# Turning the expert inputs with 32x32 block transposes on VectorE in an MoE block

## The reference

```python
def clamped_swiglu_expert(xb, w_gu, b_gu, w_down, b_down):
    gu = xb @ w_gu + b_gu                      # (.., 1024) @ (1024, 2048)
    gate = jnp.minimum(gu[:, :D_FF], SWIGLU_LIMIT)
    up = jnp.clip(gu[:, D_FF:], -SWIGLU_LIMIT, SWIGLU_LIMIT)
    act = (up + 1.0) * (gate * jax.nn.sigmoid(gate * SWIGLU_ALPHA))
    return act @ w_down + b_down               # (.., 1024) @ (1024, 1024)
...
# top 4 of 32 experts for each token; the output is the gated sum over a token's 4 experts
```

## Time and profile before

| | |
|---|---|
| time of three runs, us | 1556.98, 1557.81, 1560.6 (median 1557.81) |
| span of the profiled execution, us | 1561.2 |
| TensorE busy in matmuls | 1331.3 us, 85% of the span |
| VectorE busy | 461.4 us, 30% |
| ScalarE busy | 237.5 us, 15% |
| GpSimd busy | 163.4 us, 10% |
| HBM read and written | 447.69 MB and 28.44 MB |

### The profile page before, as it was taken

One profiled execution on the slowest core, in us unless ns is written; L12 is line 12 of the kernel. 1 busy time (PEld: TensorE's weight loads), 2 busy tenths in 40 slices (PEclk: granted clock), 3 DMA queues, 4 the chain that ended last, 5 costly groups with the idle time before them and its releaser, 6 DMA issues.

```text
span 1561.2 us, 31310 instructions
## 1 busy us (share of the span) xinstructions
PE 1331.3 (85%) x12575; PEld 639.3 (41%) x12576; DVE 461.4 (30%) x1076; ACT 237.5 (15%) x514; POOL 163.4 (10%) x269
## 2 busy tenths in 40 slices
PE   7999969998689888878989999989889767998881
PEld 6754459955433333332333333323333222333330
DVE  1247695342322212222212222212222121221226
ACT  3145453421011000000000100000000000010000
POOL 3000040000410000000000100001000000100031
PEclk9999999999699999999999999999999988999985
DMA  8721002075699999999979899899979999969955
GB/s 304 232 73 61 21 35 55 2 297 225 260 353 379 403 376 418 400 388 370 393 316 391 335 368 355 338 404 416 389 315 413 417 416 398 399 279 402 402 216 201
DMA packets 117336, 476.85 MB, mean 305 GB/s; under 512 B 8388, under 2 KB 42228, under 8 KB 84532
## 3 DMA queue, kind: packets, MB, share of 16 engines
q1 hardware_dynamic: 99792, 444.50, 72.0%
q0 software_dynamic: 6816, 21.24, 3.7%
q10 hardware_dynamic: 10692, 10.62, 2.0%
HBM read 447.69 MB, written 28.44 MB: 305 GB/s over the span
## 4 chain that ended last, share of the span: by engine, by line
DMA 59%; PE 25%; DVE 6%; SPq 5%; issue 2%; another core or an unknown queue 1%; ACT 1%; ACTq 1%; DVEq 0%; POOLq 0%; POOL 0%
DMA y_scratch<-Y 55%; PE PS L749 14%; PE PS L1129 4%; PE PSC L749 3%; PE PS L1149 3%; DMA BDN<-in_expert_b_down 2%; DVE Y L1541 2%; SPq L297 2%; SPq L264 2%; DMA W<-in_w_in 1%; DVE W L1580 1%; SPq L279 1%; PE PS L979 1%; DMA XG<-hn_scratch,IDXC 1%
## 5 line engine op out<-in xcount | busy, mean ns | idle before, releaser
L1129 PE MATMUL PS<-W,XT 128*32 128x512 f32 x5184 | 602.4, 606 | 37.6 <-DVE GU L1521 30.5
L1149 PE MATMUL PS<-W,AT 128*32 128x256 f32 x5184 | 335.3, 411 | 112.0 <-ACT AT L710 106.6
L1129 PEld LDWEIGHTS PS<-W,XT 128*32 128x32 f32 x5184 | 160.9, 111 | 374.4 <-issue 364.1
L1149 PEld LDWEIGHTS PS<-W,AT 128*32 128x32 f32 x5184 | 176.0, 118 | 298.7 <-ACT AT L710 149.3
L749 PE MATMUL PS<-W 128*128 128x512 f32 (+6 forms) x1068 | 274.3, 415 | 9.9 <-DMA W<-in_w_in 4.0
L749 PEld LDWEIGHTS PS<-W 128*128 128x128 f32 (+1 forms) x1068 | 173.4, 196 | 90.9 <-issue 74.2
L1541 DVE TENSOR_TENSOR Y<-PS,BDN 128x256 f32<-128x256 f32 x81 | 34.4, 425 | 579.8 <-DMA y_scratch<-Y 552.2
L710 ACT ACTIVATE AT<-PS 128x256 f32<-128x256 f32 x81 | 31.1, 384 | 839.3 <-issue 597.4
L1521 DVE TENSOR_TENSOR GU<-PS,BGU 128x512 f32<-128x512 f32 x81 | 56.0, 692 | 195.5 <-PE PS L1129 180.2
L465 POOL COPY IDXC<-IDX 128x1 uint32 (+1 forms) x82 | 15.0, 183 | 929.1 <-PE PS L1110 923.4
L468 POOL DMA_INDIRECT XG<-hn_scratch,IDXC x82 | 80.1, 977 | 64.6 <-POOL IDXC L465 64.6
(11 more groups left out here) (238 smaller groups left out, 652.5 us busy)
## 6 DMA issues: line engine op xcount, KB each, us to landing
W<-in_expert_w_gate_up SPq DMA_DIRECT2D x128, 2048.0 KB, 13.5
W<-in_expert_w_down SPq DMA_DIRECT2D x64, 2048.0 KB
y_scratch<-Y ACTq DMA_DIRECT2D x79, 128.0 KB
W<-in_w_in SPq DMA_DIRECT2D x9, 1024.0 KB, 6.4
y_scratch<-AT SPq DMA_DIRECT2D x1, 8704.0 KB
W<-in_x SPq DMA_DIRECT2D x8, 512.0 KB, 4.9
y_last_scratch<-AT SPq DMA_DIRECT2D x1, 2560.0 KB, 39.2
W<-in_w_in SPq DMA_DIRECT2D x2, 1040.0 KB, 11.0
```

What stands on the lines that cost most here:

```text
L1129: last = pe.matmul(GPS[32 * j:32 * j + 32, :].rearrange("p (g n) -> p g n", g=2), XT[:, (k % 2) * P + (k // 2) * 32:(k % 2) * P + (k // 2) ...
L1149: last = pe.matmul(DPS[32 * j:32 * j + 32, :], AT[:, (k % 2) * P + (k // 2) * 32:(k % 2) * P + (k // 2) * 32 + 32], DNW[p][:, k, j * QW:(j ...
```

## The change

- XG is turned by one VectorE transpose of 32x32 blocks (x_turn) straight from SBUF to SBUF. It stands in activate(i), behind the clamp of the gate, and turns X of block i+1. The four TensorE transposes of a block and the two ScalarE copies are gone.
- The activations are turned in the same way at the end of activate(i), behind a wait until down(i-1) has ended, since AT is a single tile.
- The source is read with a stride of 8 elements, so that partition 32j + f of chunk c holds row 8(32j + f) + c. The weights therefore lie as (p k): partition p holds rows 8p to 8p + 7 of the matrix. What one copy puts in one partition (2 rows of 8 KB of gate-up, 4 rows of 4 KB of down) is now one run of 16 KB in HBM and in SBUF. The number of copies (6 for an expert) and their order and waits are as before.
- y_evac, y_store, the single tile Y and their waits are the same. The store is now not behind at_copy on ScalarE, and down(i) gets AT from VectorE.

```diff
+NC = QW // 32
...
-        GPS, DPS, XPS, ATPS, RPS = PS[0], PS[1][:, 0:QW], PS[2][:, 0:QW], PS[3][:, 0:QW], PS[6][:, 0:P]
+        GPS, DPS, RPS = PS[0], PS[1][:, 0:QW], PS[6][:, 0:P]
+        XGV = XG[:, :].rearrange("p (f c) -> p c f", c=NC)
+        XTV = XT[:, :].rearrange("p (c f) -> p c f", c=NC)
+        ACTV = GU[:, 0:QW].rearrange("p (f c) -> p c f", c=NC)
+        ATV = AT[:, :].rearrange("p (c f) -> p c f", c=NC)
...
-                                 w_gu[e].rearrange("(k p) n -> p k n", p=P)[:, 2 * q:2 * q + 2, :]).then_inc(S_(f"gu_in{p}{q}"), 16)
+                                 w_gu[e].rearrange("(p k) n -> p k n", p=P)[:, 2 * q:2 * q + 2, :]).then_inc(S_(f"gu_in{p}{q}"), 16)
...
-                                 w_dn[e].rearrange("(k p) n -> p k n", p=P)[:, 4 * q:4 * q + 4, :]).then_inc(S_(f"dn_in{p}{q}"), 16)
+                                 w_dn[e].rearrange("(p k) n -> p k n", p=P)[:, 4 * q:4 * q + 4, :]).then_inc(S_(f"dn_in{p}{q}"), 16)
...
             def next_gather(i):
-                g.wait_ge(S_("xt_ps"), i)
+                g.wait_ge(S_("xt_ready"), i)
...
             def block_step(i, dst, row):
-                at_copy(i - 1)
-                a.wait_ge(S_("xt_ps"), i + 2)
-                a.wait_ge(S_("gu_ps"), i + 1)
-                xt_copy(i + 1)
                 sigmoid(i)
                 y_store(i - 1, dst, row)
...
-                    if k == 5:
-                        pe.wait_ge(S_("gathered"), (i + 2) * 16)
-                        x_transposes(i + 1)
-                        if not first:
-                            pe.wait_ge(S_("act_ready"), i)
-                            act_transposes()
...
-                                         XT[:, (k % 2) * P + (k // 2) * 32:(k % 2) * P + (k // 2) * 32 + 32], rhs,
+                                         XT[:, 32 * k:32 * k + 32], rhs,
...
-                                         AT[:, (k % 2) * P + (k // 2) * 32:(k % 2) * P + (k // 2) * 32 + 32],
+                                         AT[:, 32 * k:32 * k + 32],
...
+            def x_turn(i):
+                v.wait_ge(S_("gathered"), (i + 1) * 16)
+                v.transpose(XTV, XGV).then_inc(S_("xt_ready"), 1)
             def activate(i, p, first):
                 v.wait_ge(S_("gu_ps"), i + 1)
                 if not first:
-                    v.wait_ge(S_("at_ps"), i)
+                    v.wait_ge(S_("at_ready"), i)
                 tt(GU[:, :], GPS, BGU[p][:, :], ALU.add).then_inc(S_("gu_evac"), 1)
                 v.wait_ge(S_("gu_evac"), i + 1)
                 ts(GU[:, 0:QW], GU[:, 0:QW], LIMIT, None, ALU.min).then_inc(S_("gate_ready"), 1)
+                x_turn(i + 1)
...
                 stt(out=GU[:, 0:QW], in0=GU[:, QW:2 * QW], scalar=1.0, in1=SIG[:, :], op0=ALU.add, op1=ALU.mult).then_inc(S_("act_ready"), 1)
+                v.wait_ge(S_("act_ready"), i + 1)
+                v.wait_ge(S_("d_ps"), i + 1)
+                v.transpose(ATV, ACTV).then_inc(S_("at_ready"), 1)
```

More of the change, by code:

```diff
@@ L339, in _ @@
                 sp.dma_start(GUW[0][:, 2 * q:2 * q + 2, :],
-                             w_gu[0].rearrange("(k p) n -> p k n", p=P)[:, 2 * q:2 * q + 2, :]).then_inc(S_(f"gu_in0{q}"), 16)
+                             w_gu[0].rearrange("(p k) n -> p k n", p=P)[:, 2 * q:2 * q + 2, :]).then_inc(S_(f"gu_in0{q}"), 16)
             for t in range(NT):
@@ L696, in _ @@
             nb = last + 1
-            def xt_copy(i):
-                a.activation(XT[:, :], XPS, ACT.Copy).then_inc(S_("xt_ready"), 1)
             def sigmoid(i):
@@ L705, in sigmoid @@
                 a.activation(SIG[:, :], GU[:, 0:QW], ACT.Sigmoid, scale=ALPHA).then_inc(S_("sig_ready"), 1)
[L707 to L710, removed]
             def y_store(i, dst, row):
@@ L718, in _ @@
             f = a.value_load(LASTB[0:1, NE - 2:NE - 1], min_val=NE - 2, max_val=MAXB - 1) + 1
[L719 to L723, removed]
             sigmoid(0)
@@ L741, in _ @@
                     block_step(f + 1 + j, yl_d, j * BT)
-            at_copy(last)
             y_store(last, yl_d, (last - f) * BT)
@@ L1104, in _ @@
                 last.then_inc(S_("list_ps"), 1)
[L1106 to L1111, removed]
             def gate_up(i, p, rnd, first_of_expert, first):
@@ L1133, in gate_up @@
                         last.then_inc(S_(f"gu_read{k // 2}" if k < KD - 1 else "gu_ps"), 1)
[L1135 to L1138, removed]
             def down(i, p, rnd):
@@ L1171, in _ @@
             pe.transpose(RPS, ident[:, :], ident[:, :]).then_inc(S_("d_ps"), 1)
-            x_transposes(0)
             gate_up(0, 0, 16, True, True)
@@ L1189, in _ @@
             last = expert(NE - 1, 1, last, NE * 8, NE * 8)
-            pe.wait_ge(S_("act_ready"), last + 1)
-            act_transposes()
             down(last, 1, NE * 8)
@@ L1543, in _ @@
             v.memset(IDXC[:, 1:2], 0).then_inc(S_("y_ready"), 1)
+            x_turn(0)
             spread_biases(0, 0, 32)
```

## The result

The changed kernel takes 1679.24 us (median; 1673.81 to 1683.27), the kernel before took 1557.5 us beside it. The ratio is 1.077, with a 95% interval of 1.074 to 1.081: 122 us slower. The profiled execution has a span of 1678.3 us, 117.1 us more than that of before.

A forecast was written before the change was run, and what follows sets the result against it. The prediction took waits for stores of Y as the bound, DMA engines second. Longer store waits added 212 us over 29 experts and VectorE transposes 5: span 1561.2 + 217 = 1778, median 1775 us, range 1600 to 1900.

The forecast's parts named there:

- Rival (a): Waits of store packets for weight pieces double in the expert stage: 1775 us, own range 1690 to 1890; chance 0.68.
- (b): Store packets wait longer, but weight loads fill the gaps: 1561 + 0 to 100, about 1620 us; chance 0.12.
- The ring and its price: y_evac, store, landing, next y_evac: each store packet waits for one weight piece, 0.65 us at 16 KB, store turn 26.3 us.
- Four engines with 33 packets: A store of Y, 132 packets, was read as four DMA engines with 33 packets each.
- The walk through an expert of two blocks: Step-by-step timing of stores against loads: 42 slow packets, 39.2 us for each expert; at best 33, at worst 42.4.
- Experts of three blocks: First store quick, the next two meet 26 and 14 weight pieces: 44.8 us for each of 13 experts.
- The start of the stage: The start of the expert stage, with little loading, was left unchanged.
- Transposes on VectorE: Two for each block, 0.45 us each; on the path for one store in three at most, 12 us; 5 us taken.
- Relief of TensorE and ScalarE: Transposes off TensorE (0.82 us each block) and copies off ScalarE (down some 1.5 us sooner): counted as nothing.
- Clock: TensorE's clock falls behind long waits: 2.7 us for each of 29 experts, up to 78 us, most hidden by the store.
- Rival (c): DMA engines take turns by volume, so stores beside any weights take the present gate-up time: 1650 us; chance 0.05.
- Rival (d): Faster: weights arrive in the old pieces, or 16 KB pieces are served in parts others pass between: 1540 us; chance 0.10.

The follow-up runs named there:

- `pieces_8_4`: The changed kernel with weight copies cut into pieces of 8 KB (gate-up) and 4 KB (down), all else as changed: 1542.9 us, ratio 0.989 to the kernel before.
- `before_pk`: The kernel before with only the weights loaded as (p k), in pieces of 16 KB; output not the layer's: 1704.07 us, ratio 1.091.
- `y4`: The changed kernel with the store of Y as four copies, one for each quarter, 32 rows outermost: 1447.37 us, ratio 0.928 to the kernel before.
- `y2`: The changed kernel with the store of Y as two copies of two quarters each: 1792.36 us in one run, beside 1560.09 for the kernel before.
- `turns_twice`: The changed kernel with each VectorE transpose issued twice, the second behind a wait for the first: 1694.18 us, ratio 1.0955 to the kernel before.
- `pieces_4`: The changed kernel with all weight copies cut into pieces of 4 KB: 1555.98 us, ratio 0.998 to the kernel before.

## Why the prediction was right in kind and too high in size

Rival (a) was forecast, at 1775 us; 1679 us were measured, inside the range of 1600 to 1900, with 122 us of loss for 217. That is 11 us below the own range of (a), 1690 to 1890, and above the 1661 us at which (b) ends. The mechanism was right, and the walk was mis-sized; that the time still lies inside the range owes something to the width of the range and to errors that went opposite ways, as told below.

- *The ring and its price.* Right, shown by `pieces_8_4`, `before_pk` and `y4`. A store packet beside 16 KB was put at 0.65 us and took 0.598; a store beside weights all the way was put at 26.3 us, and most of the late intervals are 24 to 25. One reading was off without weight: rows 7 have 30 busy slices and not 32, 2.25 us and not 2.4.
- *Four engines with 33 packets.* Right, shown by `y4` and `y2`.
- *The walk through an expert of two blocks* is the step that was mis-sized. It had 42 slow packets and 39.2 us; measured are 32.2 us in the mean of 13 such experts, less even than its lower bound of 33. That is 92 of the 107 us by which the sum over the 29 experts (1224) lies above the 1116.6 measured. Two things in it were off. It let the first store's packets start at 4.5 us, and the part of 3.9 us from issue to first packet is that of stores issued while loads are in flight; with empty queues the first packets came 1.2 us behind the issue (698.07 to 699.3), and all 132 were through 3.4 us behind it (701.5), just ahead of the first pieces of the gate-up copies that SyncE issued at 700.86. And the down copies don't wait for the late y_evac: down of the expert's last block needs the evacuation before it, and that store was quick, so it ran at 679.56 beside the late store, and the down copies followed the gate-up copies without a gap. So one load meets one store: 24.6 + 7 = 31.6 us.
- *Experts of three blocks* were put at 44.8 us and took 43.8 in the mean. Eleven of the 13 take 41.4 in the mean, near 24.6 + 7 + 10.4 = 42.0: here the second slow store of the walk was missing too, and TensorE's pace of 10.4 us stood in its place. Two have two late stores, and take 57.6 and 55.6 us. So the closeness of the mean is in part luck. In all the 29 experts cost +105 us, not +212.
- *The start of the stage* was left unchanged and is 10.5 us later (494.0 for 483.55 us).
- *Transposes on VectorE.* 0.45 us was taken, 0.65 measured, within the bounds. Counted with 5 us in all; `turns_twice` shows 15 to 28 us for the same again, since 40 of the 81 evacuations now wait for no store. The step "one store in three at most" was wrong. The gathers were in time, as foreseen: x_turn waited 0.6 us for them in 74 blocks.
- *Relief of TensorE and ScalarE.* Taken as nothing. Together, with the transposes on VectorE paid, they are worth 16 us with the old pieces and 25 (22 by the ratios) with the new. One part can be seen: down follows y_evac within 0.1 us (697.47 + 0.42 to 697.99) and not 1.39 us behind the issue.
- *Clock.* That it would fall behind the long waits was foreseen, and that the store hides most of it was not borne out. Down behind the late store took 5.81 us instead of 3.64, at a granted clock of 0.50 (1.2 GHz) until 702 us. TensorE had stood idle for 7.9 us before it:

```profile
697.00:700.00 3.00, 2.01 (x20) 1.15 (x24) 1.87 (x5) 0.42 (x1) 0.00 (x0) 0.50 0.12 39
```

  The store beside it was quick, y_evac waited for this down (697.99 + 5.81, the transpose, y_evac at 704.53), and so the 2.2 us were paid in the short interval of 7 us. About 2 us for each of 29 experts are some 60 us. This is an estimate from the timeline, and no run tried it by itself. If it holds, it is a term that the sum put at nothing and that offset part of the walk's excess.
- *Rival (b)*, loads that fill the gaps: only a part of it came. The gate-up and down copies of one load flow without a gap, but between loads the engines stand idle, and the DMA share fell to 0.82.
- *Rival (c)*, turns by volume: a store beside pieces of 16 KB would have stayed at 16.3 us. It took 24.6. The Trainium skill (DMA: Bandwidth & Descriptors, Queues, rings and completion order) says that an engine drains a packet of about 9 to 17 descriptors from one queue before it switches to the next. The runs don't show how many store packets pass in one turn. They show an exchange of about one for one in number: 127/4 = 32 store packets for each of four engines, beside 451/16 = 28 packets of 8 KB and more for each of the 16, from 678 to 697 us.
- *Rival (d)* is out as well: the pieces were 16 KB, and store packets waited for each.
- DMA share: forecast 0.78, measured 0.82. The new stride of the weights didn't slow them: `y4` moved 424 GB/s. TensorE's wait ahead of down: forecast over 250 us, measured 286.8.

## What to carry to other kernels

In this kernel a small transfer that shared the DMA engines with bulk loads took its packets on one engine times the time of one bulk piece, at pieces of 4, 8 and 16 KB. Longer runs in the bulk loads then made it slower, though no byte was added. So look whether a ring of waits hangs on a small transfer before merging runs. Then give the small transfer a shape that spreads it over all 16 engines: here that one edit turned a loss of 7.7% into a gain of 7.2%, and with it the large pieces did no harm. The same edit brings 5.7% without the change, so it was the first thing to mend.

## What the runs showed of the hardware that was not expected

- From issue to first packet, a store took 3.9 us while weights were in flight (673.84 to 677.7) and 1.2 us with empty queues (698.07 to 699.3). Of 20 stores in the trace after (561 to 738 and 1334 to 1447 us), the 14 issued at a DMA share of 0.56 or more took 3.3 to 4.9 us, and the 5 issued at a share of 0.11 or less took at most 1.3 us.
- Weights flowed at 424 GB/s in pieces of 16 KB and 416 in 8 and 4 KB, with the same four store copies. With the single store copy and pieces of 4 KB it was 378, and 366 with 2 KB, at DMA shares of 0.97 and 1.00. All are of 700 to 1300 us.
- With more pieces, SyncE's issues themselves take long: two down copies 2.2 us in pieces of 16 KB and 11.3 us in pieces of 4 KB. The chain of `pieces_4` has 39% of the span on SyncE's queue. Whether the issues are slow by themselves or wait for busy DMA engines is open.
- The strided VectorE transpose of 128x256 float32 takes 630 to 668 ns, half as long again as the shuffle of the same shape.
